# First block of a two-block transformer kernel: the order of the two branches, and half of the turned rows moved from TensorE to VectorE

## The chip, the cores and the metric

One core of a Trainium2 chip (trn2) runs the whole program. The metric is the device time of one execution in microseconds (us), the median of the runs shown. Inputs and output lie in the chip's memory (HBM); all values are fp32.

## The reference, cut to what matters

Two transformer blocks run one after the other on 256 rows of 1024 columns. The change lies in the first one, behind its attention and its short convolution:

```
mixed = (jax.nn.sigmoid(gate_a) * (o_nsa @ w_branch_a)      # o_nsa: 256 x 512,  w_branch_a: 512 x 1024
         + jax.nn.sigmoid(gate_b) * (z @ w_branch_b))       # z:     256 x 1024, w_branch_b: 1024 x 1024
x = x + mixed @ w_out                                       # w_out: 1024 x 1024
h = rms_norm(x, norm2_g)
return x + jnp.square(jax.nn.relu(h @ w_up)) @ w_down
```

The second block (a long convolution, a sparse attention, a cross attention and another feed-forward part) follows and isn't touched.

## The kernel before, in words

**Products of high and low parts.** Every fp32 operand is split into a high part, which TensorE takes as fp32r, and the rest, the low part. A product is the sum of three: high x high, low x high, high x low. Weights come in as **units** of two slices of 128 x 512 (512 KB). SyncE loads a unit into one of 5 raw buffers, ScalarE copies it to the high buffer `whi` (`make_hi`, L1164, its instructions show at L1160), VectorE subtracts to get the low one, `wlo` (`make_lo`, L1756, instruction at L1766), and TensorE works it off with 12 matmuls of 512 columns (`rows`, L569). There are 5 pairs of high and low buffers, so the high part of unit u is made once unit u-5 is done; SyncE loads unit u once the low part of unit u-5 is made.

**Groups.** A group of units makes 512 output columns for both tiles of 128 rows: 4 units where the contraction is 1024 long, 2 where it is 512 long. A list written by hand gives the order of the groups, and all engines follow it. Around the change it is (units in brackets):
- `b1_ga0`, `b1_ga1`, `b1_gb0`, `b1_gb1` (36 to 51): the gates
- `b1_wa0`, `b1_wa1` (52 to 55): first branch, columns 0 to 511 and 512 to 1023
- `b1_wb0`, `b1_wb1` (56 to 63): second branch
- `b1_wo0`, `b1_wo1` (64 to 71): the output projection, whose left operand is `mixed` turned (contraction along the partitions)
- then the feed-forward part

**Side steps.** Each engine's program carries small jobs as generators, `side`: after each unit (or, on ScalarE and VectorE, at each unit of `run`, L1180 and L1771) one `next` runs the job to its next `yield`. `run` makes the last unit of a group only at the start of the next group, that is, behind the work that takes the group's result out.

**The work around the change.** Results of a group lie in two banks of PSUM. VectorE multiplies them by the gates in place of the gate (`times`, L2093: `GA` at L2100, `GB` at L2102) and adds the branches (`plus`, L2105, instruction at L2109), which counts up `mixed`: 2 when the left 512 columns are there, 4 when all are. TensorE turns `mixed` by 128 x 128 transposes into PSUM (`turn_tiles`, L717, instruction at L723), eight for the left half (steps j = 0 and 1) and eight for the right one (j = 2 and 3). ScalarE copies the high part out of PSUM into `XT` (`make_t_hi`, L1223), VectorE makes the low part (`make_t_lo`, L1825, instruction at L1836). `b1_wo0` needs step j with its unit j.

In the kernel before, the left half is mixed behind `b1_wb0`, and TensorE turns it behind the second unit of `b1_wb1`; the right half is mixed behind `b1_wb1`, and TensorE turns it behind the first unit of `b1_wo0` (L742 to L750), waiting there for `mixed` at 4:

```
for j in range(2, 4):
    e.wait_ge(mixed, 4)
    turn_tiles(T_M1, j, GB)
```

VectorE also sums the squares of the memory rows for a later norm (`mean_both`, L1797, first instruction L1801); GpSimd raises them to the power -1/2 (`norm_both`, L2608), and VectorE makes two diagonal tiles of the result (`DR`, L1842). The squares themselves are ScalarE's (L1217).

The functions below are the ones the change touches, and what calls them.

Of the kernel before, what the change touches and what calls it, by code (L numbers as in the profile page):

```python
# [10 lines left out]
ALU = mybir.AluOpType  # L11
# [29 lines left out]

END_PARTS = (((1, 1, 0, 512), (1, 2, 512, 1024)), ((0, 1, 0, 320), (1, 3, 640, 1024), (0, 2, 320, 640)))

TURN = {s: i for i, s in enumerate((T_M1, T_2, T_MIX, T_M2, T_XA, T_FFN))}
GAIN = {T_X: "norm1", T_MEM: "normmem", T_2: "norm2", T_MIX: "normmix", T_XA: "normx", T_FFN: "normffn"}
TAPS2 = (4, 4, 2, 4, 4, 4, 6, 0, 7, 3, 6, 3, 3, 7, 4, 5, 3, 5, 0, 8, 0, 1, 3, 1, 0, 0, 1, 1, 3, 1, 1, 5, 5, 4, 7, 4, 5, 7, 6, 4, 8, 5, 6, 7, 5, 4, 8, 4, 1, 7, 5, 4, 5, 4, 3, 7, 0, 4, 7, 4, 9)

# [7 lines left out]
def build(nc, A, out):  # L55
    ctx = ExitStack()
    with ctx:  # L57
# [3 lines left out]
        def sem(name):  # L61
            return ctx.enter_context(nc.semaphore(name))
# [47 lines left out]
        GA = work(W0 + 12784, "GA", 2048)  # L110
        GB = work(W0 + 16240, "GB", 2048)
        XS = work(W0 + 4096, "XS", 2048)

        XG = work(W0 + 16232, "XG", 2056)
        XF = XG[:, 8:2056]
# [95 lines left out]
        for nm, o in (("ga", 4376), ("gb", 5400)):  # L211
            for i in range(2):
                group(f"b1_{nm}{i}", "rows", w_in, o + 512 * i)
        for i in range(2):
            group(f"b1_wa{i}", "rows", A["w_branch_a"], 512 * i, kts=4)
        for i in range(2):
            group(f"b1_wb{i}", "rows", A["w_branch_b"], 512 * i)
        for i in range(2):
            group(f"b1_wo{i}", "rows", A["w_out"], 512 * i)

# [160 lines left out]
        qg_made = sem("q_gains_made")  # L381
        pair_done, o_hi, o_lo = sem("pair_summed"), sem("o_hi_made"), sem("o_lo_made")
        z_hi, z_lo = sem("z_hi_made"), sem("z_lo_made")
        gate, mixed = sem("gates_made"), sem("mixed")
        right, h_sq, h_hi, h_lo = sem("right_half_copied"), sem("h_squared"), sem("h_hi_made"), sem("h_lo_made")
        ix_done, ix_relu, ix_sum, sel_made = sem("index_scores"), sem("index_relu"), sem("index_summed"), sem("selection")
        wi_t, wi_out, ki_moved, kw_zero = sem("wi_turned"), sem("wi_copied"), sem("ki_moved"), sem("kw_zeroed")
# [119 lines left out]
        def tensor_program(e):  # L507
# [233 lines left out]

            def turn_block1():  # L742
                yield
                for j in range(2):
                    e.wait_ge(mixed, 2)
                    turn_tiles(T_M1, j, GB)
                for _ in range(3):
                    yield
                for j in range(2, 4):
                    e.wait_ge(mixed, 4)  # L750
                    turn_tiles(T_M1, j, GB)
                yield
                e.wait_ge(t_lo, t_at[T_M1, 0])
                e.wait_ge(dr_made, 4)
                mm(PB[4][:, 0:256], ones, DR[:, :], True, True).then_inc(rx_done, 1)
                for _ in range(4):
                    yield
                e.wait_ge(rx_out, 2)
                for j in range(2):
                    e.wait_ge(*out_at["b1_wo0", 1])  # L760
                    turn_tiles(T_2, j, X, (t_lo, t_at[T_M1, j]))
                for _ in range(3):
                    yield
                for j in range(2, 4):
# [261 lines left out]
            for nm in ("ga", "gb"):  # L1026
                for i in range(2):
                    rows(f"b1_{nm}{i}", XT, t_ready(T_X), side)
            for i in range(2):
                rows(f"b1_wa{i}", OT, lambda kt: (o_lo, kt + 1))  # L1030
            rows("b1_wb0", ZT, lambda kt: (z_lo, kt + 1))
            side = turn_block1()
            rows("b1_wb1", ZT, lambda kt: (z_lo, kt + 1), side)
            for i in range(2):
# [117 lines left out]
        def scalar_program(e):  # L1152
# [68 lines left out]
                return XS[:, t * D + 512 * i:t * D + 512 * i + 512]  # L1221

            def make_t_hi(s, j, T):  # L1223
                e.wait_ge(*((turned, 4 * TURN[s] + j + 1) if s != T_FFN else tile_at[f"xo{j // 2}", 2 * (j % 2) + 1]))
                if s in GAIN:
                    for k in range(2):
                        kt = 2 * j + k
                        copy(T[:, kt * 512:kt * 512 + 256], PB[4 + j][:, k * 256:k * 256 + 256],
                             prm(GAIN[s], kt)).then_inc(t_hi, 1)
                else:  # L1230
                    d = T[:, 2 * j * 512:(2 * j + 2) * 512].rearrange("p (k h n) -> p k h n", k=2, h=2)
                    copy(d[:, :, 0, :], PB[4 + j][:, :].rearrange("p (k n) -> p k n", k=2)).then_inc(t_hi, 1)

            def turn_block1():
                yield
                yield
                for j in range(2):
                    make_t_hi(T_M1, j, XT)
                    yield
                yield  # L1240
                for j in range(2, 4):
                    make_t_hi(T_M1, j, XT)
                yield
                e.wait_ge(mt_in, 16)
# [334 lines left out]
            for nm, G in (("ga", GA), ("gb", GB)):  # L1579
                for i in range(2):  # L1580
                    run(f"b1_{nm}{i}", side, *([gates1()] if nm == "gb" and i else [make_z]))
                    if nm == "ga" and i == 0:
                        e.wait_ge(z_lo, 4)
                    for t in range(2):
                        g = G[:, t * D + 512 * i:t * D + 512 * i + 512]
                        if nm == "gb" and i:
                            e.wait_ge(*tile_at["b1_gb1", t])
                            e.activation(g, PB[bank_of["b1_gb1", t]][:, :], ACT.Sigmoid, scale=NR[N_X][t]).then_inc(out_a, 1)
                        else:
                            if nm == "gb":  # L1590
                                e.wait_ge(z_lo, 8)
                            copy_out(f"b1_{nm}{i}", t, g, NR[N_X][t])
            run("b1_wa0")
            run("b1_wa1")
            for i in range(2):
                for t in range(2):
                    e.wait_ge(mem_in[t], 16)
                    norm_square(N_MEM, MEM, i, t, MSQ[:, 512 * i:512 * i + 512] if t == 0 else None)
            run("b1_wb0")
            side = turn_block1()  # L1600
            for name in ("b1_wb1", "b1_wo0", "b1_wo1"):
                run(name, side)
# [141 lines left out]
        def vector_program(e):  # L1744
# [80 lines left out]
            def make_t_lo(s, j, T):  # L1825
# [7 lines left out]
                            op1=ALU.subtract).then_inc(t_lo, 1)  # L1833
                else:
                    d = T[:, 2 * j * 512:(2 * j + 2) * 512].rearrange("p (k h n) -> p k h n", k=2, h=2)
                    e.tensor_tensor(d[:, :, 1, :], PB[4 + j][:, :].rearrange("p (k n) -> p k n", k=2),  # L1836
                                    d[:, :, 0, :].bitcast(F32), ALU.subtract).then_inc(t_lo, 1)

            def turn_block1():
                for t in range(2):  # L1840
                    e.wait_ge(factor, 2 * POW[N_MEM] + t + 1)
                    e.tensor_scalar(DR[:, t * P:t * P + P], ident, NR[N_MEM][t], None, ALU.mult).then_inc(dr_made, 1)  # L1842
                yield
                yield
                for j in range(2):
                    make_t_lo(T_M1, j, XT)
                    yield
                yield
                for j in range(2, 4):
                    make_t_lo(T_M1, j, XT)  # L1850
# [236 lines left out]
            def make_z_lo(i, f):  # L2087
# [2 lines left out]
                e.tensor_tensor(ZT[:, ft * 512 + 256:ft * 512 + 512], UU[i][:, f, 2:258],  # L2090
                                ZT[:, ft * 512:ft * 512 + 256].bitcast(F32), ALU.subtract).then_inc(z_lo, 1)

            def times(name, G, i, ready, n=None):  # L2093

                for t in range(2):
                    g = G[:, t * D + 512 * i:t * D + 512 * i + 512]
                    e.wait_ge(*tile_at[name, t])
                    e.wait_ge(*ready(t))
                    if n is None:
                        e.tensor_tensor(g, PB[bank_of[name, t]][:, :], g, ALU.mult).then_inc(out_d, 1)  # L2100
                    else:
                        e.scalar_tensor_tensor(out=g, in0=PB[bank_of[name, t]][:, :], scalar=NR[n][t], in1=g,  # L2102
                                               op0=ALU.mult, op1=ALU.mult).then_inc(out_d, 1)

            def plus(name, G, i, other):  # L2105
                for t in range(2):
# [273 lines left out]
                z = make_z(i)  # L2380
            run("b1_ga0", side, z)
            now(z)
            for name in ("b1_ga1", "b1_gb0", "b1_gb1"):
                run(name, side)
            for i in range(2):
                run(f"b1_wa{i}")
                times(f"b1_wa{i}", GA, i, gate_made(0))
            mean_both(N_MEM)
            run("b1_wb0")
            times("b1_wb0", GB, 0, gate_made(2), N_X)  # L2390
            plus("b1_wb0", GB, 0, GA)
            side = turn_block1()
            run("b1_wb1", side)
            times("b1_wb1", GB, 1, lambda t: out_at["b1_gb1", t], N_X)
            plus("b1_wb1", GB, 1, GA)
            for i in range(2):
# [321 lines left out]
```

## Time and profile before

| | |
|---|---|
| median of 3 runs | 904.13 us (904.08 to 904.64) |
| the profiled execution | 904.41 us, of which the span from first to last instruction is 902.6 us |
| TensorE matmuls (PE) | busy 895.9 us, 99% of the span |
| VectorE (DVE) | busy 700.3 us, 78% |
| ScalarE (ACT) | busy 546.2 us, 61% |
| GpSimd (POOL) | busy 33.7 us, 4% |
| mean granted TensorE clock | 0.999 of 2.4 GHz |

An engine's busy time is the union of its instructions' spans. A timeline row begins with start and duration in us from the start of the span, then engine, line, operation, tiles and shapes, "x8" for eight instructions in a row, and in brackets how long the engine had sat idle before and who ended that. Instructions of one engine overlap at their ends, so what one costs in a row of them is the distance between starts.

### The profile page before, as it was taken

How to read it: one execution, taken by the hardware profiler on the slowest of the kernel's cores; microseconds unless marked ns; L12 is line 12 of the kernel's file. 1: busy time of each engine (PE TensorE's matmuls, PEld its weight loads, DVE VectorE, ACT ScalarE, POOL GpSimd, SP SyncE). 2: the span in 40 equal slices, each digit the busy share in tenths (PEclk: the TensorE clock that was granted, in tenths of full speed). 3: DMA queues.
4: the chain of work that ended last, by engine and by line, in shares of the span. 5: the costliest groups of instructions: out<-in, count | busy, mean ns of one | idle time of the engine just before them, and what ended most of it. 6: DMA issues, size and time to landing. Idle time of an engine off the chain costs nothing.

```text
span 902.6 us, 13622 instructions
## 1 busy us (share of the span) xinstructions
PE 895.9 (99%) x4978; PEld 771.1 (85%) x4978; DVE 700.3 (78%) x1342; ACT 546.2 (61%) x945; POOL 33.7 (4%) x43
## 2 busy tenths in 40 slices
PE   9999999999999999999999999999999999999997
PEld 7998877788888888888889998888889988888886
DVE  6789989767766666667998999999976786666666
ACT  7757776745644444456566657786745755744554
POOL 0400000000000000000010100100000000000000
PEclk9999999999999999999999999999999999999999
DMA  9965444665465555556798888488565377555551
GB/s 338 315 190 173 143 143 160 247 204 184 140 230 195 196 189 188 189 197 209 204 249 233 246 216 266 121 226 245 163 217 164 112 208 239 187 187 187 187 187 46
DMA packets 95634, 178.76 MB, mean 198 GB/s; under 512 B 7952, under 2 KB 18000, under 8 KB 95312
## 3 DMA queue, kind: packets, MB, share of 16 engines
q1 hardware_dynamic: 92128, 166.35, 56.6%
q0 software_dynamic: 3072, 11.01, 6.5%
q8 instruction: 40, 0.66, 0.3%
q10 hardware_dynamic: 368, 0.52, 0.2%
q14 instruction: 26, 0.21, 0.1%
HBM read 164.69 MB, written 1.05 MB: 184 GB/s over the span
## 4 chain that ended last, share of the span: by engine, by line
PE 99%; DVE 0%; issue 0%; DVEq 0%; ACT 0%; ACTq 0%
PE pb L509 97%; PE pb L513 1%; PE pb L723 1%; DVE X L2531 0%; DVE MSQ L2569 0%; DVE XS L2578 0%; ACT ST L1717 0%; DVEq L57 0%; DVE DG L2313 0%; DVE ST L2553 0%; DVE ST L2548 0%; DVEq L2530 0%; ACTq L1716 0%
## 5 line engine op out<-in xcount | busy, mean ns | idle before, releaser
L1766 DVE TENSOR_TENSOR wlo<-raw,whi 128x1024 fp32r<-128x1024 f32 (+1 forms) x278 | 329.5, 1212 | 87.3 <-ACT whi L1160 86.7
L1160 ACT ACTIVATE whi<-raw 128x1024 fp32r<-128x1024 f32 (+2 forms) x304 | 309.0, 1039 | 130.9 <-PE pb L509 119.0
L509 PE MATMUL pb<-XT,whi 128*128 128x512 f32 (+2 forms) x1264 | 285.1, 354 | 0.1
L509 PE MATMUL pb<-whi,ZO 128*128 128x512 f32 (+1 forms) x776 | 239.5, 388 | 0.0
L509 PEld LDWEIGHTS pb<-XT,whi 128*128 128x128 f32 (+1 forms) x1264 | 204.2, 189 | 23.1 <-issue 1.3
L509 PEld LDWEIGHTS pb<-whi,ZO 128*128 128x128 f32 x776 | 145.2, 188 | 29.3
L509 PE MATMUL pb<-XT,wlo 128*128 128x256 f32 (+1 forms) x1032 | 167.5, 282 | 0.0
L509 PE MATMUL pb<-whi,XT 128*128 128x512 f32 (+1 forms) x544 | 165.9, 391 | 0.0
L509 PEld LDWEIGHTS pb<-XT,wlo 128*128 128x128 f32 (+1 forms) x1032 | 153.0, 190 | 13.2
L509 PE MATMUL pb<-wlo,ZO 128*128 128x512 f32 (+1 forms) x388 | 148.8, 387 | 0.0
L509 PEld LDWEIGHTS pb<-whi,XT 128*128 128x128 f32 x544 | 101.6, 189 | 21.3 <-issue 0.9
L509 PE MATMUL pb<-wlo,XT 128*128 128x512 f32 (+1 forms) x272 | 98.8, 384 | 0.0
L2245 DVE SCALAR_TENSOR_TENSOR YC<-U,PR,YC 128x255 f32<-128x255 f32 (+14 forms) x240 | 95.0, 463 | 0.0
L509 PEld LDWEIGHTS pb<-wlo,ZO 128*128 128x128 f32 x388 | 72.9, 188 | 14.3
L2140 DVE TENSOR_TENSOR HF<-pb,RT 128x256 f32<-128x256 f32 x64 | 26.8, 419 | 43.1 <-ACT RT L1160 43.1
L509 PEld LDWEIGHTS pb<-wlo,XT 128*128 128x128 f32 x272 | 51.1, 188 | 9.5
L1160 ACT ACTIVATE RT<-pb 128x256 f32<-128x256 f32 x64 | 22.5, 374 | 55.0 <-PE pb L509 55.0
L1160 ACT ACTIVATE ZO<-HF 128x256 fp32r<-128x256 f32 x64 | 26.8, 418 | 31.1 <-DVE HF L2143 29.4
L1160 ACT ACTIVATE wlo<-raw 128x1024 fp32r<-128x1024 f32 x20 | 21.2, 1058 | 13.4 <-PE pb L509 13.4
L2143 DVE SCALAR_TENSOR_TENSOR HF<-HF 128x256 f32<-128x256 f32 x64 | 27.2, 426 | 2.2
L2132 DVE TENSOR_TENSOR ZO<-HF,ZO 128x256 fp32r<-128x256 f32 x64 | 26.9, 420 | 2.4
L2589 POOL TENSOR_TENSOR ST<-ST,CST 128x1 f32<-128x1 f32 (+4 forms) x10 | 11.1, 1112 | 461.2 <-DVE ST L1795 243.4
(253 smaller groups left out, 654.5 us busy)
## 6 DMA issues: line engine op xcount, KB each, us to landing
raw<-in_w_in SPq DMA_DIRECT2D x105, 512.0 KB, 5.0
raw<-in_w_ff SPq DMA_DIRECT2D x64, 512.0 KB, 5.6
raw<-in_w_up SPq DMA_DIRECT2D x32, 512.0 KB, 4.6
raw<-in_w_down SPq DMA_DIRECT2D x32, 512.0 KB, 4.8
wlo<-raw POOLq DMA_DIRECT2D x20, 512.0 KB, 7.2
raw<-in_w_branch_b SPq DMA_DIRECT2D x8, 512.0 KB, 5.4
raw<-in_w_out SPq DMA_DIRECT2D x8, 512.0 KB, 4.7
raw<-in_wx_kv SPq DMA_DIRECT2D x8, 512.0 KB, 5.4
```

What stands on the lines that cost most here:

```text
L509: return e.matmul(o, l, r, start=start, stop=stop, skip_group_check=True)
L513: return e.transpose(o, s, ident[0:n, 0:n])
L723: i = e.matmul(PB[4 + j][:, k * 256 + t * P:k * 256 + t * P + P], src[:, c:c + P], ident, start=k + t == 0, stop=k + t == 2, is_transpose= ...
L1160: return e.activation(o, i, ACT.Copy, scale=scale)
L1766: e.tensor_tensor(wlo[u % NW][:, 0:c], raw_tile(u)[:, 0:c], whi[u % NW][:, 0:c].bitcast(F32), ALU.subtract).then_inc(lo, 1)
L2132: e.tensor_tensor(ZT[:, a + 256:a + 512], HF[:, f, :], ZT[:, a:a + 256].bitcast(F32), ALU.subtract).then_inc(h_lo, 1)
L2140: e.tensor_tensor(HF[:, f, :], PB[bank_of[name, f]][:, 0:256], RT[:, m % 2, :], ALU.add).then_inc(out_d, 1)
L2143: e.scalar_tensor_tensor(out=HF[:, f, :], in0=HF[:, f, :], scalar=0.0, in1=HF[:, f, :], op0=ALU.max, op1=ALU.mult).then_inc(h_sq, 1)
L2245: m = e.scalar_tensor_tensor(out=y, in0=U2[:, f, 30:256 + k], scalar=prm("convw2", 8 * k + f), in1=y, op0=ALU.mult, op1=ALU.add)
L2589: return e.tensor_tensor(dst, src, mhalf(rows, n), ALU.pow)
```

## The change

1. `b1_wb0` goes in front of `b1_wa0`. The order is now `wb0` (units 52 to 55), `wa0` (56, 57), `wa1` (58, 59), `wb1` (60 to 63), `wo0`. Loads, high and low parts, matmuls and results follow it.
2. The left half of `mixed` is complete behind `b1_wa0` in place of `b1_wb0`.
3. TensorE's eight transposes of the left half are gone. VectorE turns it in sixteen instructions of 32 partitions x 256 elements, each turning 8 blocks of 32 x 32, into a new SBUF buffer `HB`: four during the first unit of `wa1`'s `run`, eight during the second, four during the second unit of `wb1`'s.
4. Right behind the last four, VectorE does `wa1`'s `times` tile by tile, with the low parts of the left half between, and then `mean_both`.
5. ScalarE copies the high parts of the left half at the last unit of `wb1`'s `run`, both at once. ScalarE's squares of the memory rows come behind `wa0`, between it and `wa1`.
6. The two `DR` tiles are made at `wb1`'s last unit instead of its first.
7. Steps 2 and 3 of the turn (the right half) stay on TensorE, at the place where they were.

The diff, cut to its core:

```diff
+BLOCKS = (T_M1, )
+TURNED = {sj: i + 1 for i, sj in enumerate((s, j) for s in (T_M1, T_2, T_MIX, T_M2, T_XA) for j in range(4)
+                                           if s not in BLOCKS or j >= 2)}
...
+        HB = work(W0 + 2608, "HB", 1024)[:, :].rearrange("p (k n) -> p k n", k=4)
...
+        group("b1_wb0", "rows", A["w_branch_b"], 0)
         for i in range(2):
             group(f"b1_wa{i}", "rows", A["w_branch_a"], 512 * i, kts=4)
-        for i in range(2):
-            group(f"b1_wb{i}", "rows", A["w_branch_b"], 512 * i)
+        group("b1_wb1", "rows", A["w_branch_b"], 512)
...
# tensor_program, turn_block1
                 yield
-                for j in range(2):
-                    e.wait_ge(mixed, 2)
-                    turn_tiles(T_M1, j, GB)
                 for _ in range(3):
                     yield
                 for j in range(2, 4):
...
# scalar_program, make_t_hi and turn_block1
+                    copy(d[:, :, 0, :], HB[:, 2 * j:2 * j + 2, :] if by_blocks else
+                         PB[4 + j][:, :].rearrange("p (k n) -> p k n", k=2)).then_inc(t_hi, 1)
...
+                yield
                 yield
                 yield
                 for j in range(2):
                     make_t_hi(T_M1, j, XT)
-                    yield
+                yield
                 yield
                 for j in range(2, 4):
...
+            run("b1_wb0", side)
+            now(side)
             run("b1_wa0")
-            run("b1_wa1")
             for i in range(2):
                 for t in range(2):
                     e.wait_ge(mem_in[t], 16)
                     norm_square(N_MEM, MEM, i, t, MSQ[:, 512 * i:512 * i + 512] if t == 0 else None)
-            run("b1_wb0")
+            run("b1_wa1")
...
# vector_program
+            def half_blocks(src, part):
+                d = HB.rearrange("p k (t n) -> p k t n", t=2)
+                v = src.rearrange("p (t k n) -> p k t n", t=2, k=8)
+                for m in range(4 * part, 4 * part + 4):
+                    a, b = m // 4 * 32, m % 4 * 32
+                    i = e.transpose(d[b:b + 32, :, :, a:a + 32], v[a:a + 32, 0:4, :, b:b + 32])
+                if part == 3:
+                    i.then_inc(t_blocks, 1)
+
+            def m1_blocks():
+                e.wait_ge(mixed, 2)
+                half_blocks(GB, 0)
+                yield
+                half_blocks(GB, 1)
+                half_blocks(GB, 2)
+                yield
+                yield
+                half_blocks(GB, 3)
+                for t in range(2):
+                    times_tile("b1_wa1", GA, 1, t, gate_made(0))
+                    make_t_lo(T_M1, t, XT)
+                mean_both(N_MEM)
+                yield
+
             def turn_block1():
+                yield
+                yield
+                yield
                 for t in range(2):
                     e.wait_ge(factor, 2 * POW[N_MEM] + t + 1)
                     e.tensor_scalar(DR[:, t * P:t * P + P], ident, NR[N_MEM][t], None, ALU.mult).then_inc(dr_made, 1)
                 yield
-                yield
-                for j in range(2):
-                    make_t_lo(T_M1, j, XT)
-                    yield
                 yield
                 for j in range(2, 4):
                     make_t_lo(T_M1, j, XT)
...
-            for name in ("b1_ga1", "b1_gb0", "b1_gb1"):
+            for name in ("b1_ga1", "b1_gb0", "b1_gb1", "b1_wb0"):
                 run(name, side)
-            for i in range(2):
-                run(f"b1_wa{i}")
-                times(f"b1_wa{i}", GA, i, gate_made(0))
-            mean_both(N_MEM)
-            run("b1_wb0")
+            now(side)
             times("b1_wb0", GB, 0, gate_made(2), N_X)
-            plus("b1_wb0", GB, 0, GA)
+            run("b1_wa0")
+            times("b1_wa0", GA, 0, gate_made(0))
+            plus("b1_wa0", GB, 0, GA)
+            blocks = m1_blocks()
+            run("b1_wa1", blocks)
             side = turn_block1()
-            run("b1_wb1", side)
+            run("b1_wb1", blocks, side)
             times("b1_wb1", GB, 1, lambda t: out_at["b1_gb1", t], N_X)
             plus("b1_wb1", GB, 1, GA)
```

## Rows read from the trace of the kernel before

**Rows 1.** The page, busy times; the waits of TensorE: us in total, times, longest us.
```profile
PE 895.9 (99%) x4978; PEld 771.1 (85%) x4978; DVE 700.3 (78%) x1342; ACT 546.2 (61%) x945; POOL 33.7 (4%) x43
...
PE pb L509 <- DVE DG L2313: 1.2, 1, 1.2
```

**Rows 2.** Timeline of TensorE: low-part matmuls around the first turn, and the second turn.
```profile
197.88 0.39 PE L509 MATMUL pb<-wlo,ZO 128*128 128x512 f32 x1
...
198.56 0.39 PE L509 MATMUL pb<-wlo,ZO 128*128 128x512 f32 x1
...
199.02 1.04 PE L723 MATMUL pb<-CST,GB 128*128 128x128 f32 x8
...
200.12 0.40 PE L509 MATMUL pb<-wlo,ZO 128*128 128x512 f32 x1
...
208.07 1.03 PE L723 MATMUL pb<-CST,GB 128*128 128x128 f32 x8
```

**Rows 3.** Timeline of VectorE, from the first branch's last tile to the right half's low parts.
```profile
182.89 0.69 DVE L2100 TENSOR_TENSOR GA<-pb,GA 128x512 f32<-128x512 f32 x1 [0.67 <-PE pb L509]
183.50 0.15 DVE L1801 TENSOR_TENSOR ST<-ST 128x2 f32<-128x2 f32 x1
...
183.84 2.36 DVE L1766 TENSOR_TENSOR wlo<-raw,whi 128x1024 fp32r<-128x1024 f32 x2
...
193.77 0.75 DVE L2102 SCALAR_TENSOR_TENSOR GB<-pb,ST,GB 128x512 f32<-128x512 f32 x1 [0.61 <-PE pb L509]
194.44 1.28 DVE L2109 TENSOR_TENSOR GB<-GB,GA 128x512 f32<-128x512 f32 x2
195.64 1.22 DVE L1766 TENSOR_TENSOR wlo<-raw,whi 128x1024 fp32r<-128x1024 f32 x1
196.78 0.47 DVE L1842 TENSOR_SCALAR DR<-CST,ST 128x128 f32<-128x128 f32 x2
197.17 2.35 DVE L1766 TENSOR_TENSOR wlo<-raw,whi 128x1024 fp32r<-128x1024 f32 x2
...
205.55 0.75 DVE L2102 SCALAR_TENSOR_TENSOR GB<-pb,ST,GB 128x512 f32<-128x512 f32 x1 [0.61 <-PE pb L509]
206.22 1.28 DVE L2109 TENSOR_TENSOR GB<-GB,GA 128x512 f32<-128x512 f32 x2
...
209.69 1.28 DVE L1836 TENSOR_TENSOR XT<-pb,XT 128x512 fp32r<-128x512 f32 x2
```

**Rows 4.** VectorE's transposes: all of two lines (ns min/median/max), and timeline rows with neighbours.
```profile
L2027 DVE STREAM_TRANSPOSE PT<-SM x48: 358/370/375, 128.0 to 163.1; 32x192 f32<-32x192 f32 x48
...
L1981 DVE STREAM_TRANSPOSE KCT<-KCN x4: 199/202/204, 59.4 to 60.1; 32x32 f32<-32x32 f32 x4
...
145.72 1.23 DVE L1766 TENSOR_TENSOR wlo<-raw,whi 128x1024 fp32r<-128x1024 f32 x1
146.98 1.90 DVE L2027 STREAM_TRANSPOSE PT<-SM 32x192 f32<-32x192 f32 x5
...
722.16 2.50 DVE L1897 STREAM_TRANSPOSE BT<-pb 128x512 f32<-128x512 f32 x4
```

**Rows 5.** Timeline of ScalarE: squares of the memory rows, high parts, high part of step 0.
```profile
179.12 0.61 ACT L1217 ACTIVATE MSQ<-MEM 128x512 f32<-128x512 f32 x1
...
181.58 1.04 ACT L1160 ACTIVATE whi<-raw 128x1024 fp32r<-128x1024 f32 x1
...
185.67 1.06 ACT L1160 ACTIVATE whi<-raw 128x1024 fp32r<-128x1024 f32 x1 [1.66 <-PE pb L509]
...
199.65 0.60 ACT L1160 ACTIVATE XT<-pb 128x512 fp32r<-128x512 f32 x1 [2.04 <-PE pb L723]
```

**Rows 6.** Timeline of GpSimd: the power of the memory norm.
```profile
184.07 1.54 POOL L2589 TENSOR_TENSOR ST<-ST,CST 128x2 f32<-128x2 f32 x1 [127.24 <-DVE ST L1803]
```

**Rows 7.** TensorE's last matmul, and a later stretch: busy per engine (x), clock, DMA.
```profile
896.89 0.28 PE L509 MATMUL pb<-whi,ZO 128*128 128x256 f32 x1
...
901.00:902.60 1.60, 0.00 (x0) 0.00 (x0) 0.00 (x0) 0.00 (x0) 0.00 (x0) 0.53 0.42 160
```

More of the change, by code:

```diff
@@ L42 @@
 END_PARTS = (((1, 1, 0, 512), (1, 2, 512, 1024)), ((0, 1, 0, 320), (1, 3, 640, 1024), (0, 2, 320, 640)))
-TURN = {s: i for i, s in enumerate((T_M1, T_2, T_MIX, T_M2, T_XA, T_FFN))}
+BLOCKS = (T_M1, )
+TURNED = {sj: i + 1 for i, sj in enumerate((s, j) for s in (T_M1, T_2, T_MIX, T_M2, T_XA) for j in range(4)
+                                           if s not in BLOCKS or j >= 2)}
 GAIN = {T_X: "norm1", T_MEM: "normmem", T_2: "norm2", T_MIX: "normmix", T_XA: "normx", T_FFN: "normffn"}
@@ L383, in build @@
         z_hi, z_lo = sem("z_hi_made"), sem("z_lo_made")
-        gate, mixed = sem("gates_made"), sem("mixed")
+        gate, mixed, t_blocks = sem("gates_made"), sem("mixed"), sem("half_turned_by_blocks")
         right, h_sq, h_hi, h_lo = sem("right_half_copied"), sem("h_squared"), sem("h_hi_made"), sem("h_lo_made")
@@ L1028, in tensor_program @@
                     rows(f"b1_{nm}{i}", XT, t_ready(T_X), side)
+            rows("b1_wb0", ZT, lambda kt: (z_lo, kt + 1), side)
             for i in range(2):
                 rows(f"b1_wa{i}", OT, lambda kt: (o_lo, kt + 1))
-            rows("b1_wb0", ZT, lambda kt: (z_lo, kt + 1))
             side = turn_block1()
@@ L1223, in make_t_hi @@
             def make_t_hi(s, j, T):
-                e.wait_ge(*((turned, 4 * TURN[s] + j + 1) if s != T_FFN else tile_at[f"xo{j // 2}", 2 * (j % 2) + 1]))
+                by_blocks = s in BLOCKS and j < 2
+                e.wait_ge(*((t_blocks, BLOCKS.index(s) + 1) if by_blocks else (turned, TURNED[s, j]) if s != T_FFN else
+                            tile_at[f"xo{j // 2}", 2 * (j % 2) + 1]))
                 if s in GAIN:
@@ L1231, in make_t_hi @@
                     d = T[:, 2 * j * 512:(2 * j + 2) * 512].rearrange("p (k h n) -> p k h n", k=2, h=2)
-                    copy(d[:, :, 0, :], PB[4 + j][:, :].rearrange("p (k n) -> p k n", k=2)).then_inc(t_hi, 1)
+                    copy(d[:, :, 0, :], HB[:, 2 * j:2 * j + 2, :] if by_blocks else
+                         PB[4 + j][:, :].rearrange("p (k n) -> p k n", k=2)).then_inc(t_hi, 1)
             def turn_block1():
+                yield
                 yield
@@ L1835, in make_t_lo @@
                     d = T[:, 2 * j * 512:(2 * j + 2) * 512].rearrange("p (k h n) -> p k h n", k=2, h=2)
-                    e.tensor_tensor(d[:, :, 1, :], PB[4 + j][:, :].rearrange("p (k n) -> p k n", k=2),
+                    e.tensor_tensor(d[:, :, 1, :], HB[:, 2 * j:2 * j + 2, :] if s in BLOCKS and j < 2 else
+                                    PB[4 + j][:, :].rearrange("p (k n) -> p k n", k=2),
                                     d[:, :, 0, :].bitcast(F32), ALU.subtract).then_inc(t_lo, 1)
+            def half_blocks(src, part):
[20 more added lines that the diff above has]
+                yield
             def turn_block1():
+                yield
+                yield
+                yield
                 for t in range(2):
@@ L2091, in make_z_lo, with times_tile @@
                                 ZT[:, ft * 512:ft * 512 + 256].bitcast(F32), ALU.subtract).then_inc(z_lo, 1)
+            def times_tile(name, G, i, t, ready, n=None):
+                g = G[:, t * D + 512 * i:t * D + 512 * i + 512]
+                e.wait_ge(*tile_at[name, t])
+                e.wait_ge(*ready(t))
+                if n is None:
+                    e.tensor_tensor(g, PB[bank_of[name, t]][:, :], g, ALU.mult).then_inc(out_d, 1)
+                else:
+                    e.scalar_tensor_tensor(out=g, in0=PB[bank_of[name, t]][:, :], scalar=NR[n][t], in1=g,
+                                           op0=ALU.mult, op1=ALU.mult).then_inc(out_d, 1)
             def times(name, G, i, ready, n=None):
                 for t in range(2):
[L2096 to L2103, printed above, removed]
+                    times_tile(name, G, i, t, ready, n)
             def plus(name, G, i, other):
```

## The prediction, made before the changed kernel ran

> **What bounds the kernel now.** I read the page first: TensorE's matmuls are busy 895.9 of 902.6 us, and its list of waits has one entry, 1.2 us at the very start [rows 1]. So TensorE is the bound from end to end and waits for nobody around the change; the other engines' idle time is free. Two things alone can move the time: work taken from TensorE, and a wait given to it.
>
> Then I read TensorE's timeline. Its rhythm is one low-part matmul every 0.68 us (197.88, 198.56), three matmuls each; a unit of 12 takes 2.72 us. The turn at 199.02 breaks it once: the next low-part matmul comes at 200.12 where the rhythm has 199.24, so eight transposes cost 0.88 us. The second turn stands at 208.07 [rows 2]. Last I read VectorE's timeline for how much room it leaves ahead of that second turn: `plus` of the right half ends at 206.22 + 1.28 = 207.50, and TensorE asks for it at 208.07 [rows 2, 3]. The room there is 0.57 us, though VectorE had idle stretches before it.
>
> **What is removed.** Eight of TensorE's transposes: 0.88 us, all on the path. Nothing else of TensorE's work changes; the order of the groups moves equal units about. The most the change can gain is so 0.88 us, 0.1% of 904.13.
>
> **What is added.** Sixteen transposes on VectorE, of 32 x 256. The trace has none of this size. It has 370 ns for 32 x 192 and 202 ns for 32 x 32, a slope of 168 / 160 = 1.05 ns an element, which gives 437 ns for 256; five of the 192 kind take 1.90 us, so their starts lie (1.90 - 0.37) / 4 = 0.38 apart, 0.01 more than one takes: they don't overlap [rows 4]. I take 0.449 us each, 7.18 us for sixteen. Bounds: the four of 128 x 512 overlap, (2.50 - 0.68) / 3 = 0.61 apart, taking as long alone as the `plus` of that size, and 256 elements fewer make that 0.34, 5.4 us in all; in proportion to the elements it would be 0.38 x 256 / 192 = 0.51, 8.2 us [rows 3, 4]. I take the value between, because it comes from the same shape of 32 partitions. Beside that, a low part ahead of a transpose that doesn't start at partition 0 costs 1.26 us instead of 1.14 (145.72 to 146.98, against 195.64 to 196.78) [rows 3, 4]; that happens twice: 0.24.
>
> The Trainium skill speaks against this edit: VectorE: DVE Perf Modes, Rules for kernel authors, sends a 128 x 128 transpose to TensorE where PSUM will do as its destination. The trace agrees in price, 0.88 us there against my 7.18 here. The same page's section The three transpose paths has 311 ns for VectorE on 128 x 128 in bf16; eight such would be 2.5 us (an estimate from that page), and the sum would come out as the third rival below.
>
> **Where VectorE must be done.** TensorE asks for the right half at 208.07 - 0.88 = 207.19 in the new kernel. VectorE's work ahead of that is tied at its other end to the last tile of `wa0`. That group now ends two units behind the place where `wa1` ended, so the tile VectorE took at 182.89 is taken at 182.89 + 5.44 = 188.33 [rows 3]. From there VectorE runs in program order, and I find no idle time in it:
> - `times` of that tile 0.61 (182.89 to 183.50), two `plus` 1.20 (194.44 to 195.64)
> - six low parts, units 61 to 66, at 1.14: 6.84
> - sixteen transposes 7.18, and 0.24
> - `wa1`'s two `times` 1.22, the low parts of steps 0 and 1 at 0.60 (1.28 for two of 0.68): 1.20; a wait of 0.07 for ScalarE's first high part, which takes 0.60 where VectorE's `times` takes 0.61 [rows 5]
> - `mean_both` 0.34 (183.50 to 183.84), `DR` 0.39 (196.78 to 197.17)
> - `wb1`'s `times` 2 x 0.67 (193.77 to 194.44), `plus` 1.28
>
> The sum is 21.91 us, all durations from [rows 3] unless said: `mixed` is full at 188.33 + 21.91 = 210.24. How long TensorE takes to wake is not in the trace; between nothing and the 0.27 of a lone transpose (eight take 1.04, 0.11 apart) [rows 2] I take 0.14, so the turn starts at 210.38. **The new wait is 210.38 - 207.19 = 3.19 us.** In the room from 188.33 to 207.19, 18.86 us, VectorE had to do 14.5 us anyway; 7.4 more don't fit.
>
> **What costs nothing.** ScalarE's high parts stay ahead: unit 61's is made behind the squares of the memory rows, which take 181.58 - 179.12 = 2.46; begun at 183.9 they end near 186.4 instead of letting unit 61 start at 185.67, and VectorE wants it at 190.1 [rows 5]. If that cover went, each 0.1 us of it would be VectorE's. The power of the memory norm takes GpSimd 1.54 us, starting 0.14 behind the mean [rows 6]; the mean ends at 204.9, so `DR` at 207.2 finds it there by 0.6. SyncE's loads follow the low parts and come up to 7 us later (unit 65's low part is made at 206.1 rather than 199.5), but unit 70's high part isn't wanted before unit 65 is done, behind 213. The left half's low part of step 0: transposes done at 202.1, high part at 202.7, low part at 203.5, and `wo0` starts at 208.07 - 2.72 - 0.88 = 204.47, so 1.0 us in hand. The banks of `wa1` are free at 204.0, wanted there too. Behind the turn, VectorE needs two low parts (2.3 us) before the right half's own, as before (207.4, then 209.69 [rows 3]), with TensorE's next unit as cover: late by nothing.
>
> **The sum.** -0.88 + 3.19 = +2.31 us. The profiled execution is 904.41 with a span of 902.6; its span would become 904.9. Against the median of 904.13, which is 0.28 below that execution, I forecast **906.4 us**. 0.2%, about what a measurement of this kernel can tell from no change, is 1.8 us: slower begins at 905.9, so the forecast is only just beyond it.
>
> **Rivals.**
> 1. *Cheaper transposes, shorter wait.* The wait shrinks with each 0.1 us of a transpose by 1.6 us. At 0.38 (as for 192 elements) the time is 905.3, at 0.34 (overlapping) 904.7: within 0.2%. For it: the four of 128 x 512 overlap; my chain has twenty terms and may be some tenths too long. Against it: 48 rows of 32 partitions that don't overlap. Chance 0.26.
> 2. *The clock falls too.* TensorE would stand still 3 us in mid-kernel, which it never does now. Its granted clock fell once in this trace: the stretch from 901.0 reads 0.53, so it was at the lower of its levels (1.2 GHz against 2.4) within 4 us of the last matmul, which ended at 897.17 [rows 7]. If it fell here and stayed down for about as long as the wait, matmuls at half speed would lose some 1.6 us more: 908.0. The Trainium skill says of the same thing (TensorE: Matmul & The Clock Gate, Part 1: The HAM clock gate) that an idle array is set to 1.2 GHz; the trace agrees. Against it: the gap is shorter than the one the trace shows. Chance 0.07, on the slower side.
> 3. *The whole gain.* VectorE is ahead of TensorE after all, and 904.13 - 0.88 = 903.2. That is the other side of my forecast: it is decided where `mixed` reaches 4, and it wants VectorE 3.2 us faster, that is transposes of 0.25 us or less. For it: VectorE has 18.86 - 14.5 = 4.4 us to spare there. Against: even the overlapping form needs 5.4. Chance 0.06. Faster by over 0.2% would need 1.8 us, more than there is to take: 0.01.
>
> The forecast itself, a wait of 2.7 us or more at full clock, has 0.60; its own range is 905.9 to 907.5, the upper end from transposes of 0.51. Slower is 0.60 + 0.07 = 0.67, same 0.26 + 0.06 = 0.32, faster 0.01. The range for 8 in 10 takes in rival 1 and half of rival 2: from 904.3 (0.34 a transpose, less 0.4 for the chain) to 908.1.
>
> **What would show it.** In the profile after: TensorE has a second entry in its waits, at L723's transposes, about 3.2 us, ended by VectorE's `plus`; the transposes of 32 x 256 take 437 ns and start 0.45 apart; VectorE has no idle time from 188.3 to 210.2; no wait at `wo0`'s first unit. I am wrong if TensorE waits under 2.7 us, if it waits at `wo0`'s first unit instead (then step 0's low part was the late one, not the right half), or if the granted clock drops below 1.0 near 210 us.

## The result and the profile after

| | before | after |
|---|---|---|
| median | 904.13 us (5 runs, 903.82 to 904.64) | 908.24 us (5 runs, 907.71 to 909.16) |
| ratio to before | | 1.0045, 95% interval 1.0034 to 1.0055 |
| profiled execution | 904.41 us, span 902.6 | 907.71 us, span 905.9 |
| mean granted clock, run by run | 0.998 to 1.000 (21 runs beside the experiments) | 0.999 in the profiled run, 0.997 in the four others |

Slower by 4.1 us, as forecast in its sign, but by 1.8 us more than the 2.3 I had worked out, and 0.14 us above the upper end of my range. The last row of the table is where the difference will turn out to lie.

The page of the changed kernel, its span, busy times and chain that ended last:

```profile
span 905.9 us, 13622 instructions
...
PE 895.9 (99%) x4970; PEld 769.4 (85%) x4970; DVE 706.8 (78%) x1358; ACT 546.5 (60%) x945; POOL 33.8 (4%) x43
...
PE 95%; DVE 3%; DMA 1%; issue 0%; SPq 0%; ACT 0%; DVEq 0%; ACTq 0%
```

TensorE's busy time is the 895.9 us of before [rows 1] in a span that is 3.3 us longer, and the chain runs through VectorE for 3% of it, the new transposes (L1850) and low parts (L1771) among it. The waits of TensorE (us in total, times, longest us):

```profile
PE pb L726 <- DVE GB L2140: 2.9, 1, 2.9
PE pb L512 <- DVE DG L2344: 1.2, 1, 1.2
```

The first line is new: TensorE stands still once around the change, at the right half's turn (L726 now), for VectorE's additions (L2140 now). VectorE's timeline of the changed kernel, from `wa0`'s second tile to those additions, answers to [rows 3]:

```profile
189.62 0.69 DVE L2127 TENSOR_TENSOR GA<-pb,GA 128x512 f32<-128x512 f32 x1 [0.67 <-PE pb L512]
190.23 1.28 DVE L2140 TENSOR_TENSOR GB<-GB,GA 128x512 f32<-128x512 f32 x2
191.43 1.22 DVE L1771 TENSOR_TENSOR wlo<-raw,whi 128x1024 fp32r<-128x1024 f32 x1
192.56 1.77 DVE L1850 STREAM_TRANSPOSE HB<-GB 32x256 f32<-32x256 f32 x4
194.35 1.23 DVE L1771 TENSOR_TENSOR wlo<-raw,whi 128x1024 fp32r<-128x1024 f32 x1
195.61 3.58 DVE L1850 STREAM_TRANSPOSE HB<-GB 32x256 f32<-32x256 f32 x8
199.20 2.36 DVE L1771 TENSOR_TENSOR wlo<-raw,whi 128x1024 fp32r<-128x1024 f32 x2
201.59 1.80 DVE L1850 STREAM_TRANSPOSE HB<-GB 32x256 f32<-32x256 f32 x4
203.43 0.69 DVE L2127 TENSOR_TENSOR GA<-pb,GA 128x512 f32<-128x512 f32 x1
204.09 0.69 DVE L1841 TENSOR_TENSOR XT<-HB,XT 128x512 fp32r<-128x512 f32 x1
204.70 0.69 DVE L2127 TENSOR_TENSOR GA<-pb,GA 128x512 f32<-128x512 f32 x1
205.30 0.68 DVE L1841 TENSOR_TENSOR XT<-HB,XT 128x512 fp32r<-128x512 f32 x1
205.90 0.15 DVE L1806 TENSOR_TENSOR ST<-ST 128x2 f32<-128x2 f32 x1
...
206.24 2.35 DVE L1771 TENSOR_TENSOR wlo<-raw,whi 128x1024 fp32r<-128x1024 f32 x2
208.51 0.47 DVE L1875 TENSOR_SCALAR DR<-CST,ST 128x128 f32<-128x128 f32 x2
208.90 1.40 DVE L2129 SCALAR_TENSOR_TENSOR GB<-pb,ST,GB 128x512 f32<-128x512 f32 x2
210.22 1.28 DVE L2140 TENSOR_TENSOR GB<-GB,GA 128x512 f32<-128x512 f32 x2
```

There is no idle time in it, as forecast: no row has a bracket behind the first. The sixteen transposes (ns min/median/max):

```profile
L1850 DVE STREAM_TRANSPOSE HB<-GB x16: 426/436/444, 192.6 to 203.0; 32x256 f32<-32x256 f32 x16
```

436 ns, where I had worked out 437, and eight of them in 3.58 us. TensorE's timeline: the first matmul of the first unit behind the gates, the turn, and the first matmul that reads `DR`, behind the next unit.

```profile
173.10 0.39 PE L512 MATMUL pb<-whi,ZO 128*128 128x512 f32 x1
...
211.56 1.09 PE L726 MATMUL pb<-CST,GB 128*128 128x128 f32 x8 [2.94 <-DVE GB L2140]
...
215.25 0.59 PE L512 MATMUL pb<-DR,CST 128*128 128x256 f32 x2
```

The first stands at 173.10, in the kernel before at 171.81: this execution was 1.29 us late before it came to anything the change touches (0.7 us of it within the first 22 us, where ScalarE waited 3.5 us in all for the first weights, 2.2 in the kernel before; the rest by 50 us). With that taken off, the turn starts at 210.27; the forecast was 210.38. TensorE would have asked at 207.19 + 1.29 = 208.48, so it lost 3.08 us; the profile's 2.9 counts from the modelled end of the last matmul. So in this one execution the sum is 1.29 - 0.88 + 3.08 = 3.49 us, and the span is longer by 3.3. Nothing in this trace explains a median of +4.1 without a late start. Two theories were left:

- **Theory 1, the clock.** The wait and the transposes make +2.2; the rest is TensorE's clock, which falls behind the wait in most executions, though not in the profiled one.
- **Theory 2, the start.** The changed program starts 1.3 us later each time.

### The profile page after: what moved, and what is told of

Same layout as the page of the kernel before. It is cut to its first block, busy times and chain, and to the rows that moved or that the text cites. A ratio compares the mean times of both kernels' runs of the same rounds, so it can differ in the third digit from the quotient of the medians.

```text
span 905.9 us, 13622 instructions
## 1 busy us (share of the span) xinstructions
PE 895.9 (99%) x4970; PEld 769.4 (85%) x4970; DVE 706.8 (78%) x1358; ACT 546.5 (60%) x945; POOL 33.8 (4%) x43
## 4 chain that ended last, share of the span: by engine, by line
PE 95%; DVE 3%; DMA 1%; issue 0%; SPq 0%; ACT 0%; DVEq 0%; ACTq 0%
PE pb L512 93%; PE pb L516 1%; PE pb L726 1%; DMA raw<-in_w_first 1%; DVE HB L1850 1%; DVE wlo L1771 1%; DVE GB L2140 0%; DVE GA L2127 0%; SPq L442 0%; DVE GB L2129 0%; SPq L445 0%; DVE XT L2350 0%; DVE wlo L2361 0%; ACT whi L1160 0%; DVE XT L1841 0%
## 5 line engine op out<-in xcount | busy, mean ns | idle before, releaser
L1771 DVE TENSOR_TENSOR wlo<-raw,whi 128x1024 fp32r<-128x1024 f32 (+1 forms) x278 | 329.4, 1212 | 87.3 <-ACT whi L1160 86.7
```

What stands on the lines that cost most here:

```text
L1771: e.tensor_tensor(wlo[u % NW][:, 0:c], raw_tile(u)[:, 0:c], whi[u % NW][:, 0:c].bitcast(F32), ALU.subtract).then_inc(lo, 1)
```

## The experiments

Times of each are medians, with the kernel before run on the same chip beside them. The interval of the ratio is a 95% one.

### The changed kernel again

> The changed kernel once more, nothing edited. Theory 1 (the clock): its wait of about 3.1 us ahead of the right half's turn costs 3.1 - 0.88 = 2.2 us, and in most executions the granted clock falls behind the wait, which costs 1.9 us more; so about 908.2 us, mean clock 0.997 in most runs. Theory 2 (the start): the changed program begins 1.3 us later every time, as its first profile has it; then the time is about 907.6 whatever the clock says, and the start shows the delay again.

908.43 us beside 904.52, ratio 1.0045 (1.0033 to 1.0058). The five runs have clocks of 0.995 to 0.997. This profile caught it. First TensorE's timeline, then stretches, each with its length, the busy time of TensorE, its weight loads, VectorE, ScalarE and GpSimd (number of instructions), and last the granted clock, the DMA's share and its rate: the wait, the first 1.2 us behind it, the next 3.4, and what follows.

```profile
171.75 0.39 PE L512 MATMUL pb<-whi,ZO 128*128 128x512 f32 x1
...
210.22 1.09 PE L726 MATMUL pb<-CST,GB 128*128 128x128 f32 x8 [2.94 <-DVE GB L2140]
...
211.78 1.05 PE L512 MATMUL pb<-whi,XT 128*128 128x512 f32 x2
212.63 0.63 PE L512 MATMUL pb<-wlo,XT 128*128 128x512 f32 x1
...
215.49 0.59 PE L512 MATMUL pb<-DR,CST 128*128 128x256 f32 x2
```

```profile
207.10:210.20 3.10, 0.17 (x1) 0.00 (x0) 3.10 (x8) 0.00 (x0) 0.00 (x0) 1.00 0.81 259
210.20:211.40 1.20, 1.18 (x10) 1.15 (x11) 1.20 (x2) 0.49 (x1) 0.00 (x0) 1.00 0.53 205
211.40:214.80 3.40, 3.40 (x10) 2.63 (x9) 3.36 (x4) 2.33 (x5) 0.00 (x0) 0.50 0.59 170
214.80:217.00 2.20, 2.20 (x11) 1.83 (x10) 0.88 (x3) 1.25 (x2) 0.00 (x0) 1.00 0.85 247
```

The start is that of before (171.75 against 171.81), so theory 2 falls. The wait is the same 3.1 us, and the clock stays at 1.00 through it; it falls to 0.50, that is 1.2 GHz, 1.2 us into the work behind it, and is back 3.4 us later. In that stretch a matmul starts every 0.43 us (two of them in 212.63 - 211.78) instead of every 0.23: 8 of them instead of 15. From the turn to the `DR` matmul it takes 215.49 - 210.22 = 5.27 us, where the first profile has 215.25 - 211.56 = 3.69: **1.58 us for the clock**, where I had expected 1.9.

### The wait without the change

In the kernel before, idle transposes in front of the right half's additions, nothing else (4, 6 or 8 of them):

```diff
             times("b1_wb1", GB, 1, lambda t: out_at["b1_gb1", t], N_X)
...
+            for m in range(8):
+                a, b = m // 4 * 32, m % 4 * 32
+                e.transpose(d[b:b + 32, :, :, a:a + 32], v[a:a + 32, 0:4, :, b:b + 32])
             plus("b1_wb1", GB, 1, GA)
```

Eight:

> The kernel before with eight transposes of 32 x 256 (into unused space) in front of the right half's additions on VectorE, nothing else. The additions are late by 8 x 0.449 = 3.6 us, less the 0.57 us of room, so TensorE waits about 3.1 us at the same place. Theory 1: +3.1 for the wait and about +1.9 for the clock in most executions, some 909.1 us with mean clocks of 0.997. Theory 2: +3.1 alone, some 907.3, clock 0.999, since the program's start is that of before.

908.36 us beside 904.52, ratio 1.0045 (1.0032 to 1.0057): a wait alone brings about a time like that of the changed kernel. That the two medians agree within 0.1 us is partly luck: this kernel still has the eight transposes on TensorE, 0.88 us, and its clock fell in fewer runs. I had put 909.1. The turn and the `DR` matmul, and the clock in stretches, of its profiled run:

```profile
211.50 1.97 PE L724 MATMUL pb<-CST,GB 128*128 128x128 f32 x8 [2.92 <-DVE GB L2110]
...
216.66 0.59 PE L510 MATMUL pb<-DR,CST 128*128 128x256 f32 x2
```

```profile
208.60:211.10 2.50, 0.00 (x0) 0.00 (x0) 2.44 (x6) 0.00 (x0) 0.00 (x0) 1.00 0.00 0
211.20:211.50 0.30, 0.00 (x1) 0.00 (x1) 0.30 (x2) 0.00 (x0) 0.00 (x0) 0.50 0.00 0
211.30:214.70 3.40, 3.20 (x12) 2.91 (x13) 3.40 (x5) 1.80 (x3) 0.00 (x0) 0.52 0.24 57
```

From turn to `DR` 5.16 us, and 0.52 for a clock behind the wait. Here the clock falls between 211.10 and 211.20, some 0.3 us before the wait ends at 211.50, so the eight transposes take 1.97 us instead of 1.09. Two of the five runs kept a mean clock of 0.999 and took 907.12 and 907.79 us; the other three took 908.36 to 909.70. The two lie where I had put "+3.1 alone" (907.3), the three 1.5 us above them in the mean. The mean clock is a coarse sign: the profiled run, where the trace shows the fall, has 0.998, and so has the profiled run of the version with the order alone (below), whose trace shows none; the clock also falls at the program's end [rows 7]. Where a run below is counted as one with a fall and has no trace, its mean clock of 0.997 or less and a time 1 to 2 us longer are all there is.

Four:

> The same with four transposes: late by 1.8 us, less 0.57 of room, a wait of about 1.3 us. Both theories: the wait is too short to bring the clock down, 904.13 + 1.3 = 905.5 us, clock 0.999. If the clock falls here too, about 907.

```profile
PE pb L724 <- DVE GB L2110: 1.1, 1, 1.1
```

905.65 us beside 904.52, ratio 1.0013 (1.0004 to 1.0022), eleven runs, none with a clock under 0.998. The wait, 1.1 us where I had expected 1.3, is paid one for one.

Six:

> The kernel before with six idle transposes ahead of the additions: a wait of 6 x 0.449 - 0.57 + 0.14 = 2.3 us. Theory 1 gives +2.3 where the clock stays and +3.8 where it falls, with more runs at the full clock than with the wait of 3.1; median near 906.8 if it stays in most. If the clock needs a wait of over 3 us, all runs are at 0.998 or above.

```profile
PE pb L724 <- DVE GB L2110: 2.0, 1, 2.0
```

906.83 us beside 904.47, ratio 1.0031 (1.0019 to 1.0042). Four runs took 906.31 to 906.97 at 0.999; two took 907.93 and 908.49 at 0.997 and 0.996. The profile is of one of the four, with the clock at 1.00 behind its wait of 2.0 us; no trace has caught the two. By their mean clocks and times, a single wait of 2.0 us is enough for the clock to fall now and then, and at 2.9 it mostly falls.

### The wait filled with work

If standing still is what brings the clock down, then work in the gap that nobody needs must make the kernel faster.

```diff
                 for _ in range(3):
                     yield
+                for _ in range(12):
+                    mm(PB[6][:, :], ZT[:, 0:P], ZT[:, 0:512], True, True)
                 for j in range(2, 4):
                     e.wait_ge(mixed, 4)
                     turn_tiles(T_M1, j, GB)
```

> The changed kernel with twelve matmuls of 512 columns ahead of TensorE's wait for the right half; their result is overwritten and nobody reads it. They take 12 x 0.227 = 2.7 us of the 3.1 us wait, so TensorE stands still for 0.4 us only and the turn starts no later. Theory 1 (the idle time brings the clock down, which costs 1.5 us): the clock stays up in all runs, and the time falls from 908.4 to about 906.8 us, by work that is added. The rival (the fall has another cause, such as the late loads or the added VectorE work, or the median is up for another reason): 908.4 as before, or more.

```profile
PE pb L726 <- DVE GB L2142: 0.2, 1, 0.2
```

```profile
210.24 1.09 PE L726 MATMUL pb<-CST,GB 128*128 128x128 f32 x8 [0.21 <-DVE GB L2142]
...
213.92 0.59 PE L512 MATMUL pb<-DR,CST 128*128 128x256 f32 x2
```

906.42 us beside 904.51, ratio 1.0022 (1.0012 to 1.0032), nine runs from 906.05 to 906.75 with no clock under 0.998. The turn starts at 210.24, as late as ever, and the `DR` matmul comes 3.68 us behind it. Twelve useless matmuls took 2 us off the median of the changed kernel (908.43 above). That settles the cause of the missing part: TensorE's idle time, by way of the clock. Against the kernel before it is +1.9 us, where my sum without the clock has +2.3; I had expected 906.8. The last 0.4 us of either difference is not explained.

### The order alone, and the transposes alone

The new order of the groups, with the left half turned by TensorE in its old place:

```diff
-BLOCKS = (T_M1, )
+BLOCKS = ()
...
                 yield
+                for j in range(2):
+                    e.wait_ge(mixed, 2)
+                    turn_tiles(T_M1, j, GB)
                 for _ in range(3):
```

> The new order of the groups alone, with the left half turned by TensorE where it was before and its low parts, the memory norm and the diagonal tiles in their old places. Both theories: no wait, no gain, 904.1 us. If the order itself cost something (loads, gates, the squares of the memory rows), it would show here as more than 904.5.

```profile
PE pb L512 <- DVE DG L2347: 1.2, 1, 1.2
```

904.32 us beside 904.52, ratio 1.0001 (0.9992 to 1.0009). Its only wait is the one at the program's start. The order costs nothing that these runs can tell.

VectorE's turn in the old order, with its transposes in two lots of eight and the low parts of steps 0 and 1 at the last unit of `wb1`'s `run`:

```diff
-        group("b1_wb0", "rows", A["w_branch_b"], 0)
         for i in range(2):
             group(f"b1_wa{i}", "rows", A["w_branch_a"], 512 * i, kts=4)
+        group("b1_wb0", "rows", A["w_branch_b"], 0)
         group("b1_wb1", "rows", A["w_branch_b"], 512)
...
+            for i in range(2):
+                run(f"b1_wa{i}")
+                times(f"b1_wa{i}", GA, i, gate_made(0))
+            mean_both(N_MEM)
+            run("b1_wb0")
             times("b1_wb0", GB, 0, gate_made(2), N_X)
-            run("b1_wa0")
-            times("b1_wa0", GA, 0, gate_made(0))
-            plus("b1_wa0", GB, 0, GA)
+            plus("b1_wb0", GB, 0, GA)
             blocks = m1_blocks()
-            run("b1_wa1", blocks)
```

> VectorE's turn of the left half in the old order of the groups (both halves of the first branch first, the low parts of steps 0 and 1 at wb1's last unit). The left half is then mixed at 195.7 instead of 191.5, and the sixteen transposes, four low parts, two low parts of the turn with their wait for ScalarE, times and additions from there end near 212.3: a wait of about 5 us, and the clock falls in every run: 904.5 - 0.9 + 5.1 + 1.5 = 910.2 us. If the order did not matter: as the changed kernel, 908.4.

Its wait, with the matmul behind it, VectorE's rows that decide it, and the clock in a stretch behind it:

```profile
PE pb L512 <- DVE wlo L1770: 4.1, 1, 4.1
...
209.73 0.47 PE L512 MATMUL pb<-whi,XT 128*128 128x512 f32 x1 [4.08 <-DVE wlo L1770]
...
206.67 2.36 DVE L1770 TENSOR_TENSOR wlo<-raw,whi 128x1024 fp32r<-128x1024 f32 x2
208.94 1.29 DVE L1840 TENSOR_TENSOR XT<-HB,XT 128x512 fp32r<-128x512 f32 x2
...
210.60:213.90 3.30, 3.30 (x10) 2.53 (x9) 3.30 (x6) 0.00 (x0) 0.00 (x0) 0.50 0.56 204
```

909.75 us beside 904.47, ratio 1.0059 (1.0046 to 1.0071); all five runs have a clock of 0.997. So the order does earn something where VectorE turns: 1.3 us or so. The place of the wait I had wrong: it is `wo0`'s first unit, and the right half is in time behind it. The profile puts the wait down to a low part of the weights, but those were done at 206.67 + 2.36 = 209.03, and TensorE starts at 209.73. What ends it is the low part of step 0, the first of the two at 208.94, done near 209.6: it comes behind all sixteen transposes and two low parts.

### Less work on VectorE ahead of the additions

Unit 66's low part, the mean and the diagonal tiles behind the additions:

```diff
-                mean_both(N_MEM)
                 yield
...
-            run("b1_wb1", blocks, side)
+            run("b1_wb1", blocks, side, held=1)
             times("b1_wb1", GB, 1, lambda t: out_at["b1_gb1", t], N_X)
             plus("b1_wb1", GB, 1, GA)
+            mean_both(N_MEM)
+            make_lo()
+            make_lo()
+            owed[0] = 0
+            for t in range(2):
+                e.wait_ge(factor, 2 * POW[N_MEM] + t + 1)
+                e.tensor_scalar(DR[:, t * P:t * P + P], ident, NR[N_MEM][t], None, ALU.mult).then_inc(dr_made, 1)
```

> The changed kernel with three jobs of VectorE put behind the right half's additions: unit 66's low part (1.14 us), the memory norm's mean (0.34) and the two diagonal tiles (0.39). Theory 1 (wait plus clock): the wait shrinks by 1.87 us to about 1.2, too short for the clock to fall: 904.5 - 0.88 + 1.2 = 904.8 us at a clock of 0.999 in all runs. That the order or the sixteen transposes cost something beyond the wait and the clock: then more than 905.5.

```profile
PE pb L726 <- DVE GB L2136: 1.1, 1, 1.1
PE pb L512 <- DVE XT L1841: 0.5, 1, 0.5
```

905.67 us beside 904.47, ratio 1.0013 (1.0004 to 1.0022); clock 0.998 or more in all eleven runs. The wait at the turn shrank as forecast, to 1.1, but what was put behind the additions stands ahead of the right half's low part, and `wo0`'s third unit waits 0.5 for that. My 904.8 left this link out; the two waits make 904.47 - 0.88 + 1.1 + 0.5 = 905.2, and the other 0.5 us of the median is not explained.

The same, and TensorE's turn moved to the middle of `wo0`'s second unit:

```diff
+            def turn_right():
+                for j in range(2, 4):
+                    e.wait_ge(mixed, 4)
+                    turn_tiles(T_M1, j, GB)
...
                     for t, k in places:
+                        if between and q == 1 and (t, k) == (0, 1):
+                            between()
```

> As defer, and TensorE turns the right half six matmuls later, in the middle of wo0's second unit. Theory 1: TensorE asks 1.36 us later, at 208.55, and the additions are there at 208.4: no wait at all, the eight transposes' 0.88 us are gained, 904.5 - 0.9 = 903.6 us, and the clock stays up. The rival: the right half's low part is then late for wo0's third unit, a wait of 0.5 us or more there, and the time is 904.2 or above.

```profile
PE pb L512 <- DVE XT L1845: 1.1, 1, 1.1
...
PE pb L512 <- DVE DR L2433: 0.5, 1, 0.5
```

905.69 us beside 904.47, ratio 1.0016 (1.0007 to 1.0025): the rival, and not my 903.6. No wait at the turn, 0.5 for `DR` and 1.1 for the right half's low part instead. VectorE is full here: putting its work in another order took 2.8 us off the changed kernel, by a shorter wait and a clock that stays up, and then named the next link. Three of the eleven runs have a clock of 0.997 and take 906.66 to 907.20.

So work has to leave VectorE. Block two makes a third of its low parts by ScalarE and a DMA that adds; three units of block one in that manner:

```diff
-        by_dma = [u for u in range(first["b2_qi"] + 1, first["b2_wa1"]) if u % 3 == 0 and u != first["b2_ki"]]
+        early = [first["b1_wb1"] + i for i in (1, 2, 5)]
+        by_dma = early + [u for u in range(first["b2_qi"] + 1, first["b2_wa1"]) if u % 3 == 0 and u != first["b2_ki"]]
...
+            for i, u in enumerate(early):
+                sum_low(i, u)
             norm_both(N_MEM)
```

> The changed kernel with the low parts of units 61, 62 and 65 made as block two makes a third of its own: ScalarE writes the negated high part, a DMA adds the raw weights. VectorE's chain to the additions is shorter by 3 x 1.14 = 3.4 us, more than the 3.1 us of wait. Theory 1: no wait at the turn, full clock, the 0.88 us of the eight transposes gained: 904.5 - 0.9 = 903.6 us. The rival: the DMA's low parts come late (7.2 us to land) and TensorE waits for one of them instead, or the raw buffers freed late hold up the loads: 905 us or more.

Beside the wait stands VectorE's row of the diagonal tiles, with its idle time:

```profile
PE pb L727 <- DVE GB L2141: 0.6, 1, 0.6
...
204.84 0.48 DVE L1876 TENSOR_SCALAR DR<-CST,ST 128x128 f32<-128x128 f32 x2 [0.61 <-POOL ST L2621]
```

904.36 us beside 904.51, ratio 1.0000 (0.9991 to 1.0009), where I had expected 903.6. The chain is 3.4 us shorter, less what comes up next: VectorE now waits 0.33 us for ScalarE's first high part of the turn, reaches `DR` before GpSimd's power is made and stands 0.61 us, and TensorE still waits 0.6. With two units (61 and 64):

> The same with two units, 61 and 64: VectorE's chain is 2.3 us shorter, a wait of about 0.8 us stays, full clock: 904.5 - 0.9 + 0.8 = 904.4 us. The rival: 905.5 or more, by waits for low parts that land late.

```profile
PE pb L727 <- DVE GB L2141: 1.0, 1, 1.0
```

904.87 us beside 904.51, ratio 1.0006 (0.9997 to 1.0015), against my 904.4; the wait is 1.0 against my 0.8. At last, three units and `DR` behind the additions:

```diff
             plus("b1_wb1", GB, 1, GA)
+            for t in range(2):
+                e.wait_ge(factor, 2 * POW[N_MEM] + t + 1)
+                e.tensor_scalar(DR[:, t * P:t * P + P], ident, NR[N_MEM][t], None, ALU.mult).then_inc(dr_made, 1)
```

> three_by_dma with the two diagonal tiles made behind the right half's additions. In three_by_dma VectorE stood still 0.61 us for the memory norm's power and worked 0.39 us on the tiles ahead of the additions, and TensorE waited 0.59 us. Without both, 1.0 us, the additions are there before TensorE asks: no wait at the turn, and the eight transposes' 0.88 us are a gain: 904.36 - 0.6 = 903.8 us, beside 904.5 of before; about 0.1%, hardly more than the measurement can tell. The rival: the next link is late by as much (the right half's low parts for wo0's third unit), and it stays at 904.4.

```profile
PE pb L513 <- DVE DG L2339: 1.2, 1, 1.2
PE pb L513 <- issue: 0.2, 1, 0.2
```

903.52 us beside 904.39, ratio 0.9992 (0.9983 to 1.0001). TensorE waits for nobody around the change any more (the 0.2 us stand at 48 us), and the difference of the medians, 0.87 us, fits what eight transposes cost. The interval reaches from 1.5 us faster to 1, so that this version beats the kernel before is likely, and not more than that.

## Why the prediction was right or wrong

- **TensorE as the bound, 0.88 us as all there is to gain: right as far as the runs can tell.** The last version, with all waits gone, is 0.87 us faster in the median, with an interval of its ratio that just takes in 1.
- **The price of a transpose: right**, 436 ns against 437, and 0.449 us from start to start ((3.58 - 0.44) / 7) as forecast, not overlapping. The slope between two sizes of the same shape was a better guide than the 128 x 512 form. All sixteen took 1.77 + 3.58 + 1.80 = 7.15 us, not the 2.5 us of my estimate from the Trainium skill's table (VectorE: DVE Perf Modes, The three transpose paths). The same page's rule to leave such a turn to TensorE (Rules for kernel authors) held here: 0.88 us there against 7.15.
- **VectorE's chain: right.** 21.91 us from 188.33 by my sum; in the profile it runs from 189.62 to 210.22 + 1.28 = 211.50, 21.88 us.
- **The wait: right in place and size**, 3.08 us against 3.19; so was the room of 1.0 us at `wo0`'s first unit: step 0's low part is done at 204.09 + 0.69 = 204.78, and the first profile has that unit's first matmul at 205.74.
- **The clock: wrong, and it is the step that failed.** The sum, -0.88 + 3.19, has no term for it: the wait was priced at full clock, and rival 2, the fall, was given 0.07, "Against: the gap is shorter than the one the trace shows." One fall, seen at the end, sets no lower bound for the gap that brings it about. What the runs show in its place is a third term of 1.5 to 1.6 us: the clock goes to 0.50 for 3.4 us around the end of the wait, and in the ten timed runs of the changed kernel nine have a mean clock of 0.997 or less. So the last of the signs of being wrong, a clock below 1.0 near 210 us, came true in the second profile. Its price was right: 1.6 us forecast (half of the wait's length; that the fall would last about as long as the wait was only a guess, and the agreement is luck: it lasts 3.4 us in three traces behind waits of 2.9, 2.9 and 4.1), 1.58 and 1.47 (5.16 - 3.69) measured, and its time of 908.0 is 0.24 from the median of 908.24.
- **The rivals on the other side** had no part in it: neither cheaper transposes nor the whole gain.
- In the sum for the median, -0.88 + 3.08 + 1.5 to 1.6 is 3.7 to 3.8 us; 3.9 to 4.1 were measured. A further 0.07 is in the traces: from the turn to the `DR` matmul takes 3.69 us behind a wait at full clock and 3.62 in the kernel before (208.07 to 211.69). The last 0.1 to 0.3 us is inside what runs differ by, and stays open.

## What to carry to other kernels

Where one engine is busy 99% of the span, lay the helper engine's work between two fixed dates on a list and compare it with the distance before anything is moved to it: 7.4 us of added work met 4.4 us of room, though VectorE was 78% busy over the whole. In this kernel a wait of TensorE of 2 to 3 us cost more than its length in 14 of 21 runs, since the clock fell around its end; when a profile shows such a wait at full clock, look at the mean clock and the time of the other runs before trusting its span. Moving jobs within a full engine won back 2.8 of 3.9 us and then named the next late link; moving them off it (here to ScalarE and a DMA) won back the rest.

## What the runs showed of the hardware that I had not expected

The clock falls near the end of the wait, and not always on the same side of it. Three traces show it: in the changed kernel it stays at 1.00 through 3.1 us of standing still and 1.2 us of work, then goes to 0.50 under full load; in the kernel before with eight idle transposes it falls 0.3 us before the wait is over; in the old order about 0.8 us behind it (209.73 to 210.5). In each it is back 3.4 us after it fell. By the mean clocks and times of the single runs it fell in 2 of 6 runs with one wait of 2.0 us, in 3 of 5 with 2.9 in the kernel before, in 9 of 10 with the changed kernel's 2.9, in 5 of 5 with 4.1, and never in eleven with 1.1. The Trainium skill (TensorE: Matmul & The Clock Gate, Part 1: The HAM clock gate) puts the lower clock down to an idle array; that filling the gap with matmuls kept the clock up in nine runs agrees. In the version with the turn half a unit later, waits of 0.5 and 1.1 us with one short piece of work between them stood beside three runs of eleven at 0.997; whether those two add up to one is not shown by a trace.

A transpose of 32 x 256 that follows a low part starts 1.13 us behind its start where it reads from partition 0 (191.43 to 192.56) and 1.26 where it doesn't (194.35 to 195.61), as in the kernel before; why was not tried.
